# Cross-attention over 256 memory tokens: a rolled loop with one score bank, against eight segments written out with two

## What is computed

```
def _memory_attention(hq, hm, wq, wkv, wo):
    q = (hq @ wq).reshape(bsz, seq, XA_HEADS, XA_HEAD_DIM)      # 4 heads of 256
    k, v = _split(hm @ wkv, [D_MODEL, D_MODEL])                 # 256 memory tokens
    ...
    s = jnp.einsum('bshd,bmhd->bhsm', q, k).astype(jnp.float32) * (XA_HEAD_DIM ** -0.5)
    p = jax.nn.softmax(s, axis=-1).astype(hq.dtype)
    o = jnp.einsum('bhsm,bmhd->bshd', p, v).reshape(bsz, seq, D_MODEL)
    return o @ wo
```

## Time and profile before

| | us |
|---|---|
| median of 3 executions (lowest, highest) | 2819.61 (2818.29, 2819.61) |
| the profiled execution, its own time | 2818.11 |
| its span, from first to last instruction | 2815.9 |
| PE busy in the span | 2753.3 |
| DVE, ACT, POOL busy | 1442.4, 847.9, 1567.8 |
| mean granted clock of TensorE, of full speed | 0.993 |

### The profile page before, as it was taken

One profiled execution on the slowest core, in us unless ns is written; L12 is line 12 of the kernel. 1 busy time (PEld: TensorE's weight loads), 2 busy tenths in 40 slices (PEclk: granted clock), 3 DMA queues, 4 the chain that ended last, 5 costly groups with the idle time before them and its releaser, 6 DMA issues.

```text
span 2815.9 us, 39727 instructions
## 1 busy us (share of the span) xinstructions
PE 2753.3 (98%) x14496; PEld 2306.6 (82%) x14496; DVE 1442.4 (51%) x1499; ACT 847.9 (30%) x1291; POOL 1567.8 (56%) x914
## 2 busy tenths in 40 slices
PE   7999999999999999999999999999999999999998
PEld 5888888888888888878988987887888888888886
DVE  7554554153556524027787866541447555553243
ACT  5333332132001112025656641111424333332222
POOL 3878775555454456645556554433044878774552
PEclk9999999999999999999999999999999999999999
DMA  3212224453222224322212113321021222224442
GB/s 134 105 67 89 89 82 157 156 210 127 105 89 97 105 98 154 125 91 71 55 35 56 50 52 127 114 78 42 0 97 68 93 79 89 73 84 174 176 157 104
DMA packets 125482, 278.36 MB, mean 99 GB/s; under 512 B 16592, under 2 KB 58704, under 8 KB 125160
## 3 DMA queue, kind: packets, MB, share of 16 engines
q1 hardware_dynamic: 103248, 215.67, 22.7%
q10 hardware_dynamic: 22168, 61.79, 5.8%
HBM read 215.46 MB, written 61.93 MB: 99 GB/s over the span
## 4 chain that ended last, share of the span: by engine, by line
PE 85%; issue 7%; POOL 4%; DVE 3%; ACT 1%; ACTq 0%; POOLq 0%; DVEq 0%
PE G L880 17%; PE G L881 17%; PE G L882 17%; PE G L964 9%; PE G L965 9%; PE G L966 9%; PE G L1222 2%; PE G L1391 1%; POOL AL L748 1%; PE G L1414 1%; PE G L1119 1%; PE G L1125 1%; DVE ylo L2562 0%; POOL rkb L723 0%; POOL Ys L708 0%
## 5 line engine op out<-in xcount | busy, mean ns | idle before, releaser
L806 POOL TENSOR_TENSOR whi<-raw,zero 128x1024 fp32r<-128x1024 f32 x129 | 249.5, 1934 | 826.1 <-PE G L882 784.2
L880 PE MATMUL G<-hhi,whi 128*128 128x512 f32 x1072 | 421.1, 393 | 17.4 <-DVE hlo L2032 17.4
L882 PE MATMUL G<-hhi,wlo 128*128 128x512 f32 x1072 | 418.6, 391 | 0.0
L881 PE MATMUL G<-hlo,whi 128*128 128x512 f32 x1072 | 418.6, 390 | 0.0
L809 POOL TENSOR_TENSOR wlo<-raw,whi 128x1024 fp32r<-128x1024 f32 x129 | 395.9, 3069 | 10.1
L2180 DVE TENSOR_TENSOR dl<-draw,dh 128x2048 fp32r<-128x2048 f32 x44 | 109.2, 2482 | 281.8 <-ACT dh L1639 281.8
L880 PEld LDWEIGHTS G<-hhi,whi 128*128 128x128 f32 x1072 | 202.0, 188 | 61.5 <-issue 15.4
L880 PE MATMUL G<-dh,whi 128*128 128x512 f32 x640 | 249.2, 389 | 0.0
L881 PE MATMUL G<-dl,whi 128*128 128x512 f32 x640 | 249.2, 389 | 0.0
L882 PE MATMUL G<-dh,wlo 128*128 128x512 f32 x640 | 249.2, 389 | 0.0
L882 PEld LDWEIGHTS G<-hhi,wlo 128*128 128x128 f32 x1072 | 202.0, 188 | 42.2
(11 more groups left out here) (443 smaller groups left out, 6507.1 us busy)
## 6 DMA issues: line engine op xcount, KB each, us to landing
draw<-a_d SPq DMA_DIRECT2D x44, 1024.0 KB, 5.8
a_d<-s SPq DMA_DIRECT2D x44, 512.0 KB, 3.0
raw<-in_wd SPq DMA_DIRECT2D x44, 512.0 KB, 3.5
raw<-in_wg SPq DMA_DIRECT2D x26, 512.0 KB, 3.9
raw<-in_wu SPq DMA_DIRECT2D x26, 512.0 KB, 4.8
raw_b<-in_wg SPq DMA_DIRECT2D x36, 256.0 KB, 3.4
raw_b<-in_wu SPq DMA_DIRECT2D x36, 256.0 KB, 4.1
x_park<-xT ACTq DMA_DIRECT2D x16, 512.0 KB, 2.6
```

The costliest lines, as they stand in the source:

```text
L806: nc.gpsimd.tensor_tensor(hi, raw[:, k, 0:w], zero[:].to_broadcast([P, w]), ALU.add).then_inc(hi_made, 1)
L880: nc.tensor.matmul(dst, wh, hi, start=start, stop=False)
L881: nc.tensor.matmul(dst, wh, lo, start=False, stop=False)
L882: return nc.tensor.matmul(dst, wl, hi, start=False, stop=stop)
```

## The change

The attention is no longer a loop. Each engine has a function `attend` that writes out all eight segments; both barriers, the copy `qs` and its semaphore are gone. PE reads the queries straight from `qT`. Scores of segment i go to `G[3]` for even i and to `G[0]` for odd i, the transposed probabilities to `G[2]`, and the output to `G[1]`. PE starts with the scores of segments 0 and 1, and gives out those of segment i+2 between the transposes and the value product of segment i. The first three heads of segment 0 wait only for the query chunks of the first six units. The wait for the keys and values (`kv_in`) moves from ACT to PE. The first unit of the `wo` product waits once per token half (`half_ready`): its first half wants the first four segments, its second half all of them.

```diff
-        def product(bank, k, tiles, hi, lo, chunk_ready=None, wh=whi, wl=wlo):
+        def product(bank, k, tiles, hi, lo, chunk_ready=None, wh=whi, wl=wlo, half_ready=None):
...
             for h in range(NHALF):
                 cols = slice(h * HALF, (h + 1) * HALF)
+                if half_ready:
+                    half_ready(h)
                 for n, t in enumerate(tiles):
...
                     product(bank, (c.unit + r) % 2, range(tiles), hi, lo,
-                            chunk_ready if first and r == 0 else None).then_inc(unit_used, 1)
+                            chunk_ready if first and r == 0 else None,
+                            half_ready=half_ready if first and r == 0 else None).then_inc(unit_used, 1)
...
-            pairs(n, chunk_ready, body)
+            pairs(n, chunk_ready or half_ready, body)
...
-        def attend(i, front, back, more=True):
-            g0, g1, g2, g3 = G
-            j = i - 1
-
-            def scores(heads):
+        def attend():
+            g1, g2 = G[2], G[1]
+
+            def scores(i, heads):
+                bank = flat(G[3 - i % 2 * 3][:])
                 for h in heads:
                     for n in range(2):
-                        last = nc.tensor.matmul(flat(g0[:])[:, h * MEM:(h + 1) * MEM], qs[:, 2 * h + n, :],
+                        last = nc.tensor.matmul(bank[:, h * MEM:(h + 1) * MEM], qT[:, 2 * h + n, i * SEG:(i + 1) * SEG],
                                                 kTx[:, 2 * h + n, :], start=n == 0, stop=n == 1)
                 return last
 
-            if front:
-                pe.wait_ge(*xp_act.at("e", i - 1))
-                pe.wait_ge(*xq_act.at("q", i))
-                scores(range(XH - 1))
-            if back:
-                pe.wait_ge(*xp_dve.at("p", j))
+            assert bank_act(c.act) is G[1] and bank_dve(c.dve) is G[2]
+            dve_bank(c.dve + 1)
+            pe.wait_ge(kv_in, (1 + RC) * 16)
+            pe.wait_ge(act_free, c.act - 2 + credit)
+            scores(0, range(XH - 1))
+            pe.wait_ge(act_free, c.act + credit)
+            scores(0, range(XH - 1, XH)).then_inc(*xp_pe.sig("S"))
+            scores(1, range(XH)).then_inc(*xp_pe.sig("S"))
+            for i in range(NSEG):
+                pe.wait_ge(*xp_dve.at("p", i))
                 for h in range(XH):
                     for m in range(2):
                         last = nc.tensor.transpose(flat(g1[:])[:, (2 * h + m) * P:(2 * h + m + 1) * P],
                                                    px[:, h, m * P:(m + 1) * P], con(C_ID))
                 last.then_inc(*xo_pe.sig("T"))
-            if front:
-                scores(range(XH - 1, XH)).then_inc(*xp_pe.sig("S"))
-            if back:
-                pe.wait_ge(*xo_dve.at("lo", j - 1))
+                if i + 2 < NSEG:
+                    pe.wait_ge(*xp_act.at("e", i))
+                    scores(i + 2, range(XH)).then_inc(*xp_pe.sig("S"))
+                pe.wait_ge(*xo_dve.at("lo", i - 1))
                 for n in range(KD):
                     if n % (KD // 2) == 0:
-                        pe.wait_ge(*xo_act.at(f"pt{n // (KD // 2)}", j))
+                        pe.wait_ge(*xo_act.at(f"pt{n // (KD // 2)}", i))
                     for m in range(2):
                         last = nc.tensor.matmul(flat(g2[:])[:, n * P:(n + 1) * P], vx[:, m, n * P:(n + 1) * P],
                                                 pxt[:, n // 2, m, :], start=m == 0, stop=m == 1)
                 last.then_inc(*xo_pe.sig("O"))
+
+        def attended(h):
+            pe.wait_ge(*xo_dve.at("lo", (h + 1) * (NSEG // 2) - 1))
...
         gemm(KD, "act", hi=ahi, lo=alo, chunk_ready=norm_chunk, after_first=lambda: norm(nt_b[:], T))
         c.norm += 4
-        barrier(pe, c)
-        pipelined(pe, attend, lambda i: None)
-        barrier(pe, c)
-        gemm(KD, "dve", hi=ahi, lo=alo)
+        attend()
+        gemm(KD, "dve", hi=ahi, lo=alo, half_ready=attended)
...
-        def next_queries(i):
-            act.wait_ge(*xp_pe.at("S", i - 1))
-            activation(qs[:], qT[:, :, bass.ds(i * SEG, SEG)], ACT.Copy).then_inc(*xq_act.sig("q"))
-
-        def attend(i, front, back, more=True):
-            g0, g1, g2, g3 = G
-            j = i - 1
-            if back:
-                act.wait_ge(*xo_pe.at("T", j))
+        def attend():
+            g1, g2 = G[2], G[1]
+
+            def exps(i):
+                bank = flat(G[3 - i % 2 * 3][:])
+                act.wait_ge(*xp_dve.at("nmx", i))
+                act.wait_ge(*xp_dve.at("p", i - 1))
+                for h in range(XH):
+                    last = activation(sx[:, h, :], bank[:, h * MEM:(h + 1) * MEM], ACT.Exp, scale=XA_SCALE,
+                                      bias=mx[:, XH + h:XH + h + 1], accum_out=mx[:, 2 * XH + h:2 * XH + h + 1])
+                last.then_inc(*xp_act.sig("e"))
+
+            exps(0)
+            for i in range(NSEG):
+                act.wait_ge(*xo_pe.at("T", i))
                 for m in range(2):
                     activation(pxt[:, 2 * m:2 * m + 2].rearrange("p h m t -> p (h m t)"), g1[:, m, :],
                                ACT.Copy).then_inc(*xo_act.sig(f"pt{m}"))
-            if front and more:
-                next_queries(i + 1)
-            if front:
-                act.wait_ge(*xp_dve.at("nmx", i))
-                for h in range(XH):
-                    last = activation(sx[:, h, :], flat(g0[:])[:, h * MEM:(h + 1) * MEM], ACT.Exp, scale=XA_SCALE,
-                                      bias=mx[:, XH + h:XH + h + 1], accum_out=mx[:, 2 * XH + h:2 * XH + h + 1])
-                last.then_inc(*xp_act.sig("e"))
-            if back:
-                act.wait_ge(*xo_pe.at("O", j))
-                activation(ahi[:, :, bass.ds(j * SEG, SEG)], flat(g2[:]).rearrange("p (k t) -> p k t", k=KD),
+                if i + 1 < NSEG:
+                    exps(i + 1)
+                act.wait_ge(*xo_pe.at("O", i))
+                activation(ahi[:, :, i * SEG:(i + 1) * SEG], flat(g2[:]).rearrange("p (k t) -> p k t", k=KD),
                            ACT.Copy).then_inc(*xo_act.sig("hi"))
...
-        act.wait_ge(kv_in, (1 + RC) * 16)
-        barrier(act, c)
-        pipelined(act, attend, next_queries)
-        barrier(act, c)
+        attend()
...
-        def attend(i, front, back, more=True):
-            S, (g0, g1, g2, g3) = xp_dve, G
-            j = i - 1
-            if front:
+        def attend():
+            S = xp_dve
+
+            def softmax(i):
+                bank = flat(G[3 - i % 2 * 3][:])
                 dve.wait_ge(*xp_pe.at("S", i))
-                nc.vector.reduce_max(mx[:, 0:XH], flat(g0[:]).rearrange("p (h m) -> p h m", h=XH),
-                                     AX_X).then_inc(*S.sig("mx"))
+                nc.vector.reduce_max(mx[:, 0:XH], bank.rearrange("p (h m) -> p h m", h=XH), AX_X).then_inc(*S.sig("mx"))
                 dve.wait_ge(*S.at("mx", i))
                 ts(mx[:, XH:2 * XH], mx[:, 0:XH], -XA_SCALE, None, ALU.mult).then_inc(*S.sig("nmx"))
                 dve.wait_ge(*xp_act.at("e", i))
                 nc.vector.reciprocal(mx[:, 3 * XH:4 * XH], mx[:, 2 * XH:3 * XH]).then_inc(*S.sig("r"))
                 dve.wait_ge(*S.at("r", i))
-                dve.wait_ge(*xo_pe.at("T", j))
+                dve.wait_ge(*xo_pe.at("T", i - 1))
                 tt(px[:], sx[:], mx[:, 3 * XH:4 * XH].unsqueeze(2).to_broadcast([P, XH, MEM]),
                    ALU.mult).then_inc(*S.sig("p"))
-            if back:
-                dve.wait_ge(*xo_act.at("hi", j))
-                cols = bass.ds(j * SEG, SEG)
-                tt(alo[:, :, cols], flat(g2[:]).rearrange("p (k t) -> p k t", k=KD), ahi[:, :, cols].bitcast(F32),
+
+            softmax(0)
+            for i in range(NSEG):
+                if i + 1 < NSEG:
+                    softmax(i + 1)
+                dve.wait_ge(*xo_act.at("hi", i))
+                cols = slice(i * SEG, (i + 1) * SEG)
+                tt(alo[:, :, cols], flat(G[1][:]).rearrange("p (k t) -> p k t", k=KD), ahi[:, :, cols].bitcast(F32),
                    ALU.subtract).then_inc(*xo_dve.sig("lo"))
...
         queries(0, KD)
-        barrier(dve, c)
-        pipelined(dve, attend, lambda i: None)
-        barrier(dve, c)
+        attend()
```

More of the change, by code:

```diff
@@ L130 @@
 WL_POOL = ["S1", "S2", "S3", "S4", "l1", "l2", "l3", "l4", "l5", "l6"]
-XQ_ACT = ["q"]
 XP_PE, XP_ACT, XP_DVE = ["S"], ["e"], ["mx", "nmx", "r", "p"]
@@ L344, in layer_kernel @@
     vx = in_h(40 * KB, "vx", [P, 2, D])
-    qs = in_h(48 * KB, "qs", [P, KD, SEG])
     sx = in_h(52 * KB, "sx", [P, XH, MEM])
@@ L435, in layer_kernel @@
     xp_pe, xp_act, xp_dve = (Steps(sem(n), x) for n, x in (("xp_pe", XP_PE), ("xp_act", XP_ACT), ("xp_dve", XP_DVE)))
-    xq_act = Steps(sem("xq_act"), XQ_ACT)
     xo_pe, xo_act, xo_dve = (Steps(sem(n), x) for n, x in (("xo_pe", XO_PE), ("xo_act", XO_ACT), ("xo_dve", XO_DVE)))
     zs_in, zm_in, rows_out, rows_in = sem("zs_in"), sem("zm_in"), sem("rows_out"), sem("rows_in")
```

(4 more changed lines are left out.)

## The result

The changed kernel takes 2804.19 us (median of 5, 2802.30 to 2805.60) against 2818.87 us for the kernel before in the same comparison (median of 5). The ratio is 0.9949, with a 95% interval of 0.9935 to 0.9964: 14.7 us, or 0.5%, shorter. The profiled execution took 2804.19 us with a span of 2802.4, 13.5 less than before.

A forecast was written before the change was run, and what follows sets the result against it. PE bounds the kernel, holding 85% of the chain; of 17.8 us idle or slow PE around the attention 5.4 stay, gaining 12.4: 2819.6 - 12.4 = 2807.2, predicted as 2807.0, range 2803 to 2813.

The forecast's parts named there:

- the stage: From the end of the last query matmul to the twelfth `wo` matmul: some 73.4 us expected where 85.8 were.
- Start: Attention's start: scores directly behind the query product, first transposes at 1957.1, PE idle 1.5 us where it lost 10.8.
- a segment stays at 8.16: Middle of the attention: each segment keeps its 8.16 us, all PE's, so the middle gains and loses nothing.
- the 65.3 of the sum: PE's full-rate work in the attention, taken as eight segments of 8.16 us.
- The jumps that go cost nothing: Middle of the attention: removing the loop's jumps gains zero, as the trace rows show no cost for them.
- The ring over DVE and ACT: Middle: from O(i) through `ahi`, `alo` and softmax to T(i+2), 7.3 us, hidden behind PE's 8.16 with 0.8 slack.
- T(6), O(6), T(7) and O(7): Transposes (T) and value products (O) of segments 6 and 7: idle 1.6 new, 1.25 and 1.0 as before.
- Clock: Both ends of the attention: granted clock stays at 1.00, no idle over 1.6 us being left.
- the first rival: At an end the clock falls after all, costing 1.9 to 2.9 us once or twice, about 2810; chance 0.25.
- a ring that binds: Middle: longer handovers make the 7.3 us exceed 8.16, costing some 3 to 4 us, 2811; chance 0.07.
- a gain given back: Behind the attention: what follows is bound by something unmoved (weights by DMA), time 2819; chance 0.04.
- code fetch stalls: Each segment: PE stalls for new code without its loop; 2825.6 at 2.3 us a segment; chance 0.09.

The follow-up runs named there:

- e1: The changed kernel with one pair of score banks and PE's order of before, still written out without barriers; 2807.62 us, ratio 0.9969 to the kernel before.
- e2: The changed kernel with both barriers of PE, ACT and DVE put back around the attention; 2809.03 us, ratio 0.9972 to the kernel before.
- e3: The kernel before with only the attention's loop over segments written out on all three engines; 2815.17 us, ratio 0.9996 to the kernel before.
- e4: The changed kernel with three heads of segment i+2's scores ahead of segment i's transposes, two bank pairs kept; 2802.98 us, ratio 0.9950 to the kernel before.
- e5: The changed kernel measured again, unaltered; 2804.63 us, ratio 0.9963 to the kernel before.
- e6: The changed kernel with 13 matmuls of unread result in the idle places of the last two segments; 2805.14 us, ratio 0.9964 to the kernel before.
- e7: The changed kernel with early `wo` tiles filling PE's idle places at the end, banks exchanged for it; 2799.87 us, ratio 0.9946 to the kernel before.
- e8: e7 with three heads of segment 2's scores also put ahead of the first transposes; 2798.49 us, ratio 0.9941 to the kernel before.

## Why the prediction was right, point by point

The forecast was 2807.0 with a range of 2803 to 2813; 2804.19 is 2.8 below it and in the range. The gain was put at 12.4 us; the stage lost 12.5 in the profile. Both ends came out as argued, but that the two numbers agree to 0.1 is luck: two misses of opposite sign cancel, 2.1 us too much for the work of the middle and 1.6 us too little for the clock. What is left is 0.3 too little for idle time and starts from idle.

- **Start.** Right: no gap ahead of the scores, first transposes expected 8.7 us after the query product and seen at 8.4, idle 1.51 for 1.5. The granted clock stayed at 1.00. e1 and e2 show two causes separately: with one bank PE waits 3.5 us, with the barrier 1.4 us. The barrier together with the `qs` copy costs 2.55 (before and e3), so 1.2 is the copy with its handover.
- **Middle.** Wrong: "a segment stays at 8.16". I took pieces of the chain that touch as proof that nothing waits there. They also contain small delays: the 12 scores of 2.76 us are 0.23 each, while 16 in a row take 3.46, or 0.216. The clue was in the earlier trace rows: 4 scores take 0.87, so 12 should take 2.61 and not 2.76. It was worth 0.26 us a segment, 2.1 against the 65.3 of the sum. Going back from after in steps, e4, e1 and e3 give the wait of the `pxt` weight load 0.15, the bank 0.04 and the loop 0.07. "The jumps that go cost nothing" was wrong by the 0.07. The ring over DVE and ACT was hidden, as forecast.
- **End.** The times of T(6), O(6), T(7) and O(7) were right: O(6) at 2.5 us after T(6) for 2.4, T(7) at 7.3 for 7.35, O(7) at 9.2 for 9.2. The barrier and the wait for `ahi` and `alo` went (2.7 in e2), and the first token half of `wo` covered them.
- **Clock.** The forecast was that it holds, and a fall was the first rival (chance 0.25, price 1.9 to 2.9). It fell in both profiled executions, over the last value product, and cost 5.44 - 3.82 = 1.6 us, by the value product at full clock behind the same idle (e2). The argument against it, that such a stretch had not lowered it before, was no argument: with the same idle times e2 and e4 kept it, and after and e5 lost it.
- **The rest.** Of the 13.5 us of span, 0.9 lies behind the stage and is not the change's: the time behind the stage is 780.8 in after, e1 and e5, and 781.7 to 782.1 in before, e2, e3, e4 and e6. In 7 us that hold the start of PE's last matmuls the clock is 0.51 before and 0.76 after:

```profile
2795.00:2802.00 7.00, 5.66 (x28) 5.58 (x28) 0.73 (x5) 0.42 (x2) 0.00 (x0) 0.51 0.00 0
```

```profile
2784.00:2791.00 7.00, 5.46 (x32) 5.28 (x32) 3.02 (x6) 0.84 (x2) 0.00 (x0) 0.76 0.00 0
```

The rivals of a ring that binds, of a gain given back and of code fetch stalls all fell: 7.90 us a segment, later stages as long as before, no idle of PE without a releaser in after or e3. The measured 14.7 us between the medians also holds some of the scatter of the kernel before, whose medians in three comparisons were 2818.87, 2816.45 and 2815.03; the later ratio of the same changed kernel is 0.9963, which is 10.4 us. The clock in the mixers, which differs between two executions of one kernel (e5), is a likely source of such scatter, not shown for the medians.

## What to carry to other kernels

Pieces of a busy engine that touch in the chain are no proof that it runs at its rate: divide a group's time by its count and compare it with the longest undisturbed group of the same form. Put independent work between a producer and the weight load that reads its result, not only enough of it to keep the engine busy (0.15 us a segment here). Where a pipeline drains, start the next product's share that is already ready; that gave e7 and e8 another 5 to 6 us for a few lines.

## What the runs showed of the hardware that I had not expected

The same idle pattern of PE in the last two segments (1.4 to 1.5, 0.94 and 0.78 us) was followed by a granted clock of 0.5 over the last value product in two profiled executions (after, e5) and not in two others (e2, e4). The shorter pattern of 1.24 and 0.78 us was followed by it in e1 and not in the kernel before and e3, where the clock fell only behind the 2.7 us of idle that come next. In e2 the same 2.69 us of idle stand there and no fall came. So in these traces the idle places alone do not tell whether the clock falls. An idle of 3.5 to 3.6 us at the start was followed by a fall in all three kernels that have it (before, e1, e3), one of 1.5 us never in five (after, e2, e5, e6, e7). At the end of the kernel the time behind the stage is 780.8 us in the three traces where the clock at the start of the last matmuls was low for 3.4 us (after, e1, e5), and 781.7 to 782.1 in the five where it was low for 6.8 us, without any change in that code.

A group of matmuls that starts from idle takes 0.2 to 0.3 us longer in the chain than one that follows other matmuls, with the granted clock at 1.00: transposes 1.09 to 1.11 for 0.87, a value product 3.82 for 3.57, scores 3.73 for 3.47. An idle place costs this on top of its own length.
